# Ten pairs of weight tiles by seven block products instead of eight pairs, with the end of the convolution branch in a new order

## The reference, cut to what matters

```python
h = rms_norm(x, g_mix) * (1.0 + sc1) + sh1
(a_q, a_k, a_v, conv_in, c_q, c_k, c_v, c_r, c_low,
 d_q, d_k, d_v, gate_logits) = jnp.split(h @ w_in, split_points, axis=-1)
# the convolution branch, of conv_in:
a, gate = jnp.split(u, 2, axis=-1)
y = a * sigmoid(gate)
y = causal depthwise convolution of width 31 + conv_b
y = silu(layer_norm(y, ln_g, ln_b))
```

## Time and profile before

| | us |
|---|---|
| median of 3 runs (1943.22 to 1945.03) | 1944.5 |
| the profiled execution | 1944.26 |
| its span, first to last instruction | 1942.5 |
| PE busy in it (98%) | 1894.2 |
| DVE busy (67%) | 1293.9 |
| ACT busy (44%) | 850.1 |

### The profile page before, as it was taken

One profiled execution on the slowest core, in us unless ns is written; L12 is line 12 of the kernel. 1 busy time (PEld: TensorE's weight loads), 2 busy tenths in 40 slices (PEclk: granted clock), 3 DMA queues, 4 the chain that ended last, 5 costly groups with the idle time before them and its releaser, 6 DMA issues. The chain is left out here.

```text
span 1942.5 us, 24191 instructions
## 1 busy us (share of the span) xinstructions
PE 1894.2 (98%) x9128; PEld 1521.4 (78%) x9128; DVE 1293.9 (67%) x1632; ACT 850.1 (44%) x1350; POOL 203.1 (10%) x120
## 2 busy tenths in 40 slices
PE   5999999999999999999999999999999999999999
PEld 4887888888766677877888778888888887888887
DVE  7699964552466576637658488678866665688855
ACT  6311243331466542175655444334454544444442
POOL 0122220000222155113100000000000000000000
PEclk8999999999999999999999999999999999999999
DMA  9465442322311151344122777401444447963343
GB/s 299 131 212 175 128 140 96 121 96 76 126 55 53 51 189 50 109 172 170 57 76 72 233 234 235 149 17 55 146 144 154 158 140 244 309 189 104 98 119 98
DMA packets 221068, 266.24 MB, mean 137 GB/s; under 512 B 12266, under 2 KB 149610, under 8 KB 220954
## 3 DMA queue, kind: packets, MB, share of 16 engines
q1 hardware_dynamic: 220830, 264.66, 42.5%
q10 hardware_dynamic: 124, 0.04, 0.0%
HBM read 187.46 MB, written 77.20 MB: 136 GB/s over the span
## 5 line engine op out<-in xcount | busy, mean ns | idle before, releaser
L939 PE MATMUL dn_ps<-h_hi,dn_hi 128*128 128x512 f32 (+1 forms) x848 | 342.5, 404 | 10.2 <-ACT dn_out L322 5.9
L941 PE MATMUL dn_ps<-h_hi,dn_lo 128*128 128x512 f32 (+1 forms) x848 | 331.4, 391 | 0.0
L940 PE MATMUL dn_ps<-h_lo,dn_hi 128*128 128x512 f32 (+1 forms) x848 | 331.2, 391 | 0.0
L305 POOL TENSOR_TENSOR dn_lo<-dn_raw,dn_hi 128x1024 fp32r<-128x1024 f32 (+1 forms) x53 | 146.4, 2763 | 657.0 <-ACT dn_hi L301 645.6
L939 PEld LDWEIGHTS dn_ps<-h_hi,dn_hi 128*128 128x128 f32 (+1 forms) x848 | 157.7, 186 | 67.3 <-issue 32.7
L941 PEld LDWEIGHTS dn_ps<-h_hi,dn_lo 128*128 128x128 f32 (+1 forms) x848 | 157.6, 186 | 36.3
L940 PEld LDWEIGHTS dn_ps<-h_lo,dn_hi 128*128 128x128 f32 (+1 forms) x848 | 157.9, 186 | 32.8 <-issue 1.2
L322 ACT ACTIVATE dn_out<-dn_ps 128x512 f32<-128x512 f32 (+1 forms) x106 | 62.5, 590 | 274.5 <-PE dn_ps L941 254.3
L1503 ACT ACTIVATE tl_ring_hi<-tl_cell 128x512 fp32r<-128x512 f32 x112 | 70.6, 631 | 146.4 <-PE mg_ps_y L941 128.3
L939 PE MATMUL mg_ps_y<-tl_ring_hi,tl_ring_hi 128*128 128x512 f32 x320 | 124.7, 390 | 0.0
L940 PE MATMUL mg_ps_y<-tl_ring_lo,tl_ring_hi 128*128 128x512 f32 x320 | 124.6, 389 | 0.0
(11 more groups left out here) (481 smaller groups left out, 4232.1 us busy)
## 6 DMA issues: line engine op xcount, KB each, us to landing
tl_raw_hidden<-hidden SPq DMA_DIRECT2D x112, 256.0 KB, 2.7
dn_raw<-w_in_dram SPq DMA_DIRECT2D x54, 512.0 KB, 4.5
ada<-w_ada_dram SPq DMA_DIRECT2D x48, 512.0 KB, 7.0
logits<-dn_out SPq DMA_DIRECT2D x64, 256.0 KB, 2.2
tl_unit<-w_up_dram SPq DMA_DIRECT2D x64, 256.0 KB, 3.2
hidden<-tl_hidden_sum SPq DMA_DIRECT2D x16, 1024.0 KB, 4.9
tl_cell<-w_down_dram SPq DMA_DIRECT2D x64, 256.0 KB, 4.8
proj<-dn_out SPq DMA_DIRECT2D x40, 256.0 KB, 2.2
```

The lines of the kernel that those rows point to most:

```text
L305: self.nc.gpsimd.tensor_tensor(self.lo_at(j), self.raw_at(j), self.hi_at(j).bitcast(F32), ALU.subtract).then_inc(self.lo_ready, 1)
L939: nc.tensor.matmul(out, w_hi[:, t, :], x_hi[:, t, :], start=begin, stop=False, skip_group_check=reopened)
L940: nc.tensor.matmul(out, w_hi[:, t, :], x_lo[:, t, :], start=False, stop=False, skip_group_check=reopened)
L941: mm = nc.tensor.matmul(out, w_lo[:, t, :], x_hi[:, t, :], start=False, stop=end, skip_group_check=reopened)
```

## The change

There are ten pairs. The two new ones are rows 30, 31 and 32, 33 (the last four of the linear attention's twelve), by the list `FIRST`. Those four are no plain tiles any more; row 17 of window attention is the only tile behind the pairs (`tail` = 1), row 16 comes ahead of them. The tiles ahead of the pairs are thus 3 to 19, the pairs come at `FIRST_TAIL` = 20, and the first gate tile is 21.

The square follows tile 15 (was 16), the variance's `statistic` tile 16 (was 17), the root tile 16 (was 18), the sigmoid tile 17 (was 19). ACT makes the high parts of T1 and T2 after tile 16 and those of T4 and T3 after tile 18 (was T1 after 16, T2 and T4 after 17, T3 after 18). The raw weights of the first pairs are loaded at j = 18 (was 19). On DVE the centring comes ahead of all token differences, the last `modulation` after difference 5, and T4's and T3's low parts after the last step of the convolution. Buffers change places: the weights' sums lie where the centred values were, their high parts where the padded input was, and three of the results where the convolution's output was.

```diff
 class Pairs:
-    COUNT = 8
+    COUNT = 10
+    FIRST = [0, 2, 4, 6, 8, 10, 12, 14, 30, 32]
...
-        self.sums = at("pr_sums", 88 * KB, [P, 4, 4, P])
-        self.hi = at("pr_hi", 64 * KB, [P, self.RING, 4, P], F32R)
+        self.sums = at("pr_sums", 64 * KB, [P, 4, 4, P])
+        self.hi = at("pr_hi", 88 * KB, [P, self.RING, 4, P], F32R)
...
-        sp.dma_start(self.raw[p % 2][:, :, :], self.dense.w_view[:, :, 2 * p * P:(2 * p + 2) * P]).then_inc(self.raw_in[p % 2], 16)
+        sp.dma_start(self.raw[p % 2][:, :, :], self.dense.w_view[:, :, self.FIRST[p] * P:(self.FIRST[p] + 2) * P]).then_inc(self.raw_in[p % 2], 16)
...
-        row = (2 * p + tile) * P
+        row = (self.FIRST[p] + tile) * P
...
-        linear = [(t * P, P, t) for t in range(R_CQ, R_DQ)]
-        window = [(t * P, P, t) for t in range(2 * Pairs.COUNT, R_CONV)]
+        linear = [(t * P, P, t) for t in range(R_CQ, Pairs.FIRST[8])]
+        window = [(t * P, P, t) for t in range(Pairs.FIRST[7] + 2, R_CONV)]
...
-        self.tail = len(window)
+        self.tail = 1
...
-    MEAN_AFTER, SQUARE_AFTER, VAR_AFTER, SWISH_AFTER = 15, 16, 18, 19
+    MEAN_AFTER, SQUARE_AFTER, VAR_AFTER, SWISH_AFTER = 15, 15, 16, 17
...
-    HIGH_AFTER = {16: (Pairs.T1,), 17: (Pairs.T2, Pairs.T4), 18: (Pairs.T3,)}
+    HIGH_AFTER = {16: (Pairs.T1, Pairs.T2), 18: (Pairs.T4, Pairs.T3)}
...
# SP
-                if j == 19:
+                if j == FIRST_TAIL - 2:
                     pairs.load(sp, 0)
                     sp.wait_ge(gated, 1)
                     pairs.load(sp, 1)
...
# PE
-                if j == VAR_AFTER - 1:
+                if j == VAR_AFTER:
                     pe.wait_ge(squared, 1)
                     statistic(sq, var_done)
...
# DVE, after the taps and the last chain
-            for n in range(1, 4):
-                difference(n)
             dve.wait_ge(mean_done, 1)
             for c in range(C):
                 ... centred (L897)
-            for n in range(4, 6):
-                difference(n)
-            low_difference(Pairs.T1)
-            for n in range(6, 10):
+            for n in range(1, 6):
                 difference(n)
             modulation(OPEN_CHUNKS + LATE - 1)
-            low_difference(Pairs.T2)
-            low_difference(Pairs.T4)
+            low_difference(Pairs.T1)
+            for n in range(6, 9):
+                difference(n)
             dve.wait_ge(rooted, 1)
             for c in range(C):
                 ... normed (L910)
-            low_difference(Pairs.T3)
             dve.wait_ge(squared, 1)
             for c in range(C):
                 ... scaled (L915)
+            low_difference(Pairs.T2)
+            difference(9)
             for c in range(C):
                 ... cv_out (L919)
+            low_difference(Pairs.T4)
+            low_difference(Pairs.T3)
+            dve.wait_ge(cv_out, C)
             for part in range(2):
                 pairs.sum_pair(dve, 0, part)
```

More of the change, by code:

```diff
@@ L90, in __init__ @@
         self.raw = [at(f"pr_raw{i}", kb * KB, [P, KT, 2 * P]) for i, kb in enumerate((48, 80))]
-        self.sums = at("pr_sums", 88 * KB, [P, 4, 4, P])
-        self.hi = at("pr_hi", 64 * KB, [P, self.RING, 4, P], F32R)
+        self.sums = at("pr_sums", 64 * KB, [P, 4, 4, P])
+        self.hi = at("pr_hi", 88 * KB, [P, self.RING, 4, P], F32R)
         self.lo = at("pr_lo", 72 * KB, [P, self.RING, 4, P], F32R)
-        self.x1, self.x5, self.u2, self.c11 = (at(f"pr_{n}", kb * KB, [P, HALF]) for n, kb in zip(("x1", "x5", "u2", "c11"), (56, 58, 60, 62)))
-        self.c22, self.c12, self.c21 = (at(f"pr_{n}", kb * KB, [P, HALF]) for n, kb in zip(("c22", "c12", "c21"), (96, 98, 100)))
+        self.x1, self.x5, self.u2, self.c11 = (at(f"pr_{n}", kb * KB, [P, HALF]) for n, kb in zip(("x1", "x5", "u2", "c11"), (96, 98, 100, 56)))
+        self.c22, self.c12, self.c21 = (at(f"pr_{n}", kb * KB, [P, HALF]) for n, kb in zip(("c22", "c12", "c21"), (58, 60, 62)))
         self.raw_in = sems(nc, ctx, "pr_raw_in0", "pr_raw_in1")
```

## The result

The changed kernel takes 1954.18 us (median of 5 runs, 1953.24 to 1955.53), the kernel before 1943.22 in 5 runs beside it: +11.0 us, a ratio of 1.0057 with a 95% interval of 1.0045 to 1.0068. It is slower, as forecast. The profiled execution took 1953.24, its span is 1951.5.

A forecast was written before the change was run, and what follows sets the result against it. PE, busy 98% of the span, was taken to bound the kernel. Pairs' start -13.3, two pairs +38.7, one tail tile -10.9, clock +2.0: +16.5 us, 1961 by the median; own range 1956 to 1965, 8 in 10 1954 to 1967.

The forecast's parts named there:

- What the matmuls save: On PE, four tiles go (-43.5 us) and two pairs come (+38.7): -4.8 us.
- DVE's idle time before `modulation`: DVE waits for the column sum after tile 17 before the last modulation, idle from 245.8 to 253.9.
- First stall: Before tile 18's first half: ACT's copy stands behind two sigmoids, so PE stands still some 6.2 us.
- `cv_out`, load 20, T4 and T3: Chain before the pairs: cv_out at 276.2, load 20 landed 284.1, ACT's high parts 288.9, T3's low part 292.2.
- The second wait: PE's wait between tile 19's end at 282 and the pairs' start at 295.7, about 13 us.
- Start of the pairs: The pairs start at 295.7 instead of 309.0 (-13.3 us), 19.3 us later than they could.
- The clock: PE's matmuls behind the second stall run at granted clock 0.50, adding 2.0 us, between nothing and 2.6.
- Pairs' pace, the tail tile: Each pair takes 19.34 us; behind them one tail tile replaces two, with its loads and stores priced at nothing.
- Nothing elsewhere, one us either way: Later stages get no other work, so no gain or loss there, with one us allowed either way.
- the transfers share: Rival, chance 0.13: transfers behind load 20 share the way, so it lands 5.3 us later: 1966.3.
- The transfer is not on the way: Rival, chance 0.08: load 20 lands before ACT asks, pairs start at 284.0: +2.8 us, 1947.3.
- The order holds: Rival, chance 0.09: cv_out comes early enough, the pairs start at 276.4, -4.8 us: 1939.7.

The follow-up runs named there:

- e8: e3 with, on DVE, the first pair's weight sums ahead of T4's low part and the first three low parts ahead of T3's: 1936.2 us.
- e7: e3 with eight pairs instead of ten, twelve tiles of the linear attention and two tail tiles: 1943.2 us.
- e2: The changed kernel with only the last modulation moved behind the convolution's last product on DVE: 1946.4 us.
- e4: The changed kernel's new order with eight pairs, twelve linear attention tiles and two tail tiles as before: 1951.0 us.
- e1: The changed kernel with SP's wait for cv_out and the store of mix moved behind load 20 and tile 18's stores: 1945.1 us.
- e6: The kernel before, run again without any edit for a second profile: 1942.3 us.
- e5: The changed kernel with SP still waiting for cv_out, but issuing load 20 ahead of mix: 1951.8 us.
- e3: The changed kernel with the edits of e1 and e2 together: 1937.3 us.

## Why the prediction was right, step by step

It was right in direction and in mechanism: both stalls, and what holds PE in each, came as forecast. The size was half as much again as measured, +16.5 for +11.0, and that the time still lies in the wide range by 0.2 us is luck. Even the low ends of the forecast's own terms together (load landed after 4 us, no matmul slowed, 1 us gained elsewhere) give 1954.6. Of the 6.8 us between 1961 and 1954.2, 1.3 come from the median before, 1944.5 when the forecast was made and 1943.2 in the runs beside the change; the rest is in the steps below.

- *What the matmuls save*, -4.8: the front of e8 against e7's gives 4.8. Right.
- *DVE's idle time before `modulation`*: 8.1 forecast, 7.99 measured, shown as a cause by e2.
- *First stall*: 6.2 forecast, 6.1 measured; that the sigmoids hold the copy stands in the rows of ACT, that it is the order's doing in e4. That it is contained in the second stall is shown by e2: it took the first away, and its gain of 7.8 is what `cv_out`, 8.2 us earlier, gives by itself.
- *`cv_out`, load 20, T4 and T3*: forecast 276.2, 284.1, 288.9, 292.2; measured from an opening that was 1.0 us earlier 274.8, 282.0, 286.7, 289.9. On the same footing (one added) this is 0.4, 1.1, 1.2, 1.3 early. The mis-sized term is the landing: 6.8 in place of 7.4. The way is shown by e1.
- *The second wait*: about 13 forecast, 10.45 measured. It starts later, as tile 19 ends at 283.7 on the same footing and not at 282 (1.5 of it is the half clock behind the first stall, which the forecast left inside the wait), and it ends 1.6 earlier, with the start of the pairs.
- *Start of the pairs*: 19.3 us late in the forecast, 17.7 in the profile (14.9 instead of 13.3 earlier than before, against 32.6 possible).
- *The clock*: 2.0 forecast; nine matmuls at 0.44 us lost 1.9, at the granted clock of 0.50 that was forecast.
- *Pairs' pace, the tail tile*: ten joins from 300.8 to 474.8 are 19.34 us apart; PE does not wait behind the pairs but for the 1.3 us that the next stage always costs. Right.
- *Sum of the front*: 16.5 forecast, 14.6 measured.
- *Nothing elsewhere, one us either way*: the step that failed in size. The medians moved 3.6 us less than the front. 3.1 of it is in the late stretch of the first profile of before, which its second profile does not have. Since there are only two profiles of before, how often it comes in either kernel stays open, and so does whether the ten pairs, by shifting all that follows, keep it away. The table speaks for some of this: all six kernels with ten pairs are 1.9 to 3.6 us better against before than their fronts say, e4 and e7 by 0.2 and -0.2. So does the spread of the executions: of 11 each, e6 and e7 lie 5.9 and 6.4 us apart, e1 and e2 3.1 and 3.5. Both speak for a loss that the kernels with eight pairs have in some executions; neither shows it.

The rivals: *the transfers share* is refuted by the changed kernel itself, whose load landed after 6.8 us and not 5.3 later than 7.4, and by e5; on this the Trainium skill ("DMA: Bandwidth & Descriptors", section "Queues, rings and completion order", descriptors are consumed in ring order) and the measurement agree. *The transfer is not on the way* became true by e1's edit, and gave +2.0 by the median (+4.2 by the front) where +2.8 was worked out for it. *The order holds* is what e3 and e8 had to make.

## What to carry to other kernels

When a stage that everything must be ready for comes earlier, compare its shift (32.6 us) with the idle time that the feeding engines have before it (17.7), and walk each in-order queue for instructions that are not needed but stand in front: here a bias of 0.2 us, a load for a tile 200 us away and a store that was not urgent held back a saving of 4.8 and cost 11. Move the waits that have late answers behind the work that is urgent; the fix took three small moves and no new resource. Half the clock behind the idle time comes on top, here 1.5 and 1.9 us for the two stalls.

## What the runs showed of the hardware

- DVE's instructions with two inputs from SBUF and POOL's low part did not run at the same time: in the kernel before `difference(5)` took 4.39 us beside it, `difference(4)` just ahead of it 2.28. A scaling with one such input was held as well, 3.60 in the kernel before and 1.53 after the change. The prediction's rule, that the second starts when the first has ended, holds for DVE here, but not always for POOL: its low part, 2.4 us by itself, stood open for 10.63 in e1 and 10.02 in e4, over several of DVE's instructions, while in e2 (255.39), beside a DVE just as busy, it took 2.48 and came in ahead of DVE's next instruction. What decides this is not shown. DVE paid 2.1 to 2.2 us in each of these cases.
- Two transfers of one issuing engine, 512 KB and 1 MB: the load took 4.4 us in front and 6.8 behind, `mix` 4.9 in front and 6.6 behind. Four loads of this size in the kernel before, away from `mix`, took 4.1 to 4.3, so being followed by `mix` cost next to nothing.
- A wait of 2.1 us late in the kernel came with a granted clock of 0.80 in its five microseconds and with eight matmuls at 0.43 us behind it; a wait of 0.5 us at the same place came with 1.00. The 1.6 us of longer waiting cost 3.1 in all. Behind the wait of 1.9 us in e1 the matmuls kept their pace (0.23 to 0.24 us, but for 0.31 to the second).
